# Layer-norm rows of the feed-forward norms spread by TensorE into PSUM, in a two-layer transformer trunk on one core

## The chip, the core and the metric

One core of a Trainium2 chip runs the whole program: TensorE (PE, with its weight loads as PEld), VectorE (DVE), ScalarE (ACT), GpSimd (POOL) and the DMA queue of SyncE (SP). The metric is the device time of one execution in microseconds (us), as the median of several runs.

## The reference

Input `x` has 512 tokens of 1024 features, in float32. There are two layers. Layer 0 mixes the tokens with a gated linear recurrence and a differential attention, layer 1 with a forgetting attention of 16 heads. What matters here is the frame around the mixers, the same in both layers:

```python
x = _layer_norm(ALPHA * x + mixer(x), ln1_g[l], ln1_b[l])
x = _layer_norm(ALPHA * x + _swiglu(x, ffn_w1[l], ffn_w2[l]), ln2_g[l], ln2_b[l])

def _layer_norm(x, g, b, eps=1e-5):
    mu = mean(x); var = mean((x - mu) ** 2)
    return (x - mu) * rsqrt(var + eps) * g + b
```

`ln1_g`, `ln1_b`, `ln2_g`, `ln2_b` are rows of 1024 numbers per layer. `_swiglu` has 2816 hidden features. So there are four layer norms, here called n1_0, n2_0 (layer 0, behind the mixer and behind the feed-forward part), n1_1 and n2_1. In the code, `norm` has them as n = 0, 1, 2, 3; the odd ones are the feed-forward norms.

## The kernel before

Tokens lie on the 128 partitions in four tiles (t = 0 to 3) of `x_res`, and features on the free axis. For every projection the activations are turned (feature on the partitions) by TensorE transposes into PSUM (`turn_tile`, L516), and each turned half tile is split into a rounded high part `xT_hi` by ScalarE (`split_hi`, L992) and a rest `xT_lo` by VectorE (`split_lo`, L1254). Weights come in chunks of up to 128x2048: SP loads a chunk into one of two raw buffers (`load`, L890), ScalarE rounds it into `w_hi` (L980), GpSimd makes the rest `w_lo` in pieces of 512 columns (L940), in a ring of three. Each product is three matmuls (`products`, L445 to L447). A chunk may be rounded when the chunk three before it has been used, and may be loaded when GpSimd is through with the chunk two before it.

The order of work on each engine is written out by hand; semaphores alone tie the engines together. PSUM banks 0 to 3 take the large products, in turn; banks 4 to 7 take transposes, attention and the products of gate and up (`h_buf`, banks 4 and 5). `open_bank` makes TensorE wait until the last reader of a bank has freed it.

Each layer ends its mixer with the projection `out{l}` and its feed-forward part with `down{l}`, both in two halves of 512 output columns. The first half is done chunk by chunk; VectorE adds it to `x_res` with `add_left` (L1434) and takes its statistics (L1435). The second half goes tile by tile in `tail_products`, and between tiles `norm_tail` places the transposes of the tiles already normed: in the n1 tails two tiles behind, in the n2_0 tail one behind. So that TensorE has work while the last tiles are normed, it also holds early pieces of the next stage: `early(0)` stands before the transposes of tile 3 and `early(1)` behind them. In the n1 tails these are the first halves of the first two gate/up products; in n2_0 they are two tiles of `foxq0` and the forget-gate product `fox_f`. `early(0)` needs tiles 0 and 1 turned and split.

VectorE does a norm tile in this order: `add_left` and statistics of the second half, aggregate (L1442), add epsilon (L1443), then `(x - mean) * gain` over 1024 columns (L1447), then it takes the root that ScalarE made meanwhile (Ln and Exp, L997 and L998), refines it with three operations on one column (L1450 to L1452), and does `x * r + bias` over 1024 columns (L1453). Behind tile t it splits tile t - 1.

The gain and bias rows lie in SBUF, broadcast to 128 partitions by DMA (512 KB each). For n1 they go to free parts of the arena, ahead of the `out{l}` chunks (L921). For n2 they go to `rows_ffn`, a part of the arena that holds hidden activations until chunk 8 of `down{l}` has been used. The SP queue waits for that use (`ffn_rows`, L905 and L907), ahead of the load of the chunk behind `down0`, and in layer 1 ahead of the output.

Of the kernel before, what the change touches and what calls it, by code (L numbers as in the profile page):

```python
# [123 lines left out]
def build(nc, w, out):  # L124
# [5 lines left out]
    with ExitStack() as ctx:  # L130
# [27 lines left out]
        level_mask = place("level_mask", [len(LEVELS), P], BF16, 2)  # L158
        small = place("small", [48], F32, 4)
# [38 lines left out]
        rows_ffn, _ = take("rows_ffn", [2, D], F32, 0)  # L198
        norm_rows = [rows_even, rows_ffn, rows_fox, rows_ffn]
# [35 lines left out]
        def named(*names):  # L235
            for n in names:
# [26 lines left out]

        n_masks = 2 + len(LEVELS)
# [10 lines left out]
                   for h in range(AH)]  # L275
        lam_loads = [(lam_rows[:, i * HD:(i + 1) * HD], w[n][0:1, :].to_broadcast([P, HD]))
# [133 lines left out]
        def _(pe):  # L410
# [121 lines left out]
            def norm_tail(tag, step, src_tiles, lag, early):  # L532

                def turn(t):

                    turn_tile(tag, t, x_res, lambda: pe.wait_ge(S["norm_done"], step * NT + t + 1),  # L540
                              4 + 2 * (t % 2))

                for t in range(NT):
                    src_tiles(t)
                    if early and t >= lag:
                        turn(t - lag)
                if early:
                    for t in range(NT - lag, NT - 1):
                        turn(t)
                    early(0)  # L550
                    turn(NT - 1)
                    early(1)
                    turned_tiles[0] += NT
# [70 lines left out]
            def swiglu(l):  # L624
# [18 lines left out]
                for i in range(6):  # L643
                    pe.wait_ge(S["h_lo"], l * NF + k0 + chunks[cs[i]][2] // 512)
                    drain(token_chunk(cs[i], "dve", hT_hi, hT_lo, k0, i == 0, (f"down{l}", 0) if i == 5 else False))
                    k0 += chunks[cs[i]][2] // 512
                k0 = 0
# [12 lines left out]
            def fox_start(i):  # L660
# [10 lines left out]
                acc = open_bank("fox_f", 4, "dve")  # L671
# [8 lines left out]
                used_with_bank(c, "fox_f")  # L680

# [202 lines left out]
        def _(sp):  # L884
# [18 lines left out]
            def ffn_rows(l):  # L903

                sp.wait_ge(*chunk_used[stage_chunks[f"down{l}"][8]])  # L905
                for i, name in enumerate(("ln2_g", "ln2_b")):
                    sp.dma_start(rows_ffn[:, i, :], w[name][l:l + 1, :].to_broadcast([P, D])).then_inc(rows_in[l], 16)  # L907

            for c in range(2, len(chunks)):
                if c == stage_chunks["down0"][-1] + 1:  # L910
                    ffn_rows(0)
                for l in range(DEPTH):
                    if c == chunk_at(f"out{l}"):
                        if l == 0:

                            sp.wait_ge(S["act_free"], 1)
                        else:

                            sp.wait_ge(S["fexp"], 3 * QUARTER)
                        for i, name in enumerate(("ln1_g", "ln1_b")):  # L920
                            sp.dma_start(norm_rows[2 * l][:, i, :], w[name][l:l + 1, :].to_broadcast([P, D])  # L921
                                         ).then_inc(rows_in[l], 16)
                load(c)
            ffn_rows(1)
# [307 lines left out]
        def _(dve):  # L1232
# [24 lines left out]

            def refine(r, var, tmp):
# [178 lines left out]
            def norm(tag, name, n):  # L1437

                for t in range(NT):
# [4 lines left out]
                    dve.wait_ge(rows_in[n // 2], 32 * (n % 2 + 1))  # L1444
                    gain, bias = (norm_rows[n][:, i, :] for i in range(2))
                    xs = x_res[:, t, :]
                    step(stt(xs, xs, st[:, 12:13], gain, ALU.subtract, ALU.mult))  # L1447
# [4 lines left out]
                    step(tt(r, r, tmp, ALU.mult))  # L1452
                    chain(stt(xs, xs, r, bias, ALU.mult, ALU.add), S["norm_done"])  # L1453
                    if t >= 1 and tag != "n2_1":
# [155 lines left out]
```

## Time and profile before

| | |
|---|---|
| median of 3 runs | 1483.52 us (1482.2 to 1485.66) |
| the profiled execution | 1485.66 us, of which 1483.9 us are its span |
| TensorE busy | 1398.3 us, 94% of the span |
| VectorE, ScalarE, GpSimd busy | 480.5, 499.9, 527.6 us |
| granted TensorE clock, mean | 0.968 of full speed |
| norms n1_0, n2_0, n1_1, n2_1 | end at about 345, 711, 1118 and 1481 us |

Times in rows are microseconds from the start of the span, unless marked ns. The ends of matmuls are modelled: the distance from start to start tells what one costs. A matmul of float32 operands stands in the trace as two instructions.

### The profile page before, as it was taken

What the parts mean: (1) busy time and instruction counts of PE and PEld (TensorE: products, weight loads), DVE (VectorE), ACT (ScalarE), POOL (GpSimd) and SP (SyncE); (2) the same over time, 40 slices, a digit from 0 to 9 for tenths busy, and PEclk for the clock granted to TensorE, in tenths of its full rate; (3) what the DMA queues carried; (4) which work ended last, traced back from release to release, by engine and by line L of the source; (5) the groups of instructions that cost most, each with busy time, mean ns of one, the idle gap of its engine ahead of it and who ended that gap; (6) DMA issues with size and microseconds to landing.
All of it is one profiled execution on the core that took longest, in us unless ns stands there. A gap on an engine that the chain in (4) does not pass through costs nothing.

```text
span 1483.9 us, 19200 instructions
## 1 busy us (share of the span) xinstructions
PE 1398.3 (94%) x7244; PEld 1174.8 (79%) x7244; DVE 480.5 (32%) x1120; ACT 499.9 (34%) x824; POOL 527.6 (36%) x421
## 2 busy tenths in 40 slices
PE   7999996799999999999899998889899999999997
PEld 6888874578888888887778887877679888888886
DVE  3366526553111111014536271533362111110005
ACT  4313236424223232112435554544323222323120
POOL 5421312044544445351342222202134454454450
PEclk9999998899999999999999999979799999999999
DMA  6311121022333233322232121012012323324231
GB/s 220 112 32 57 58 86 57 1 86 70 101 105 94 86 99 111 102 85 59 86 114 58 58 58 57 1 64 80 29 57 86 113 86 96 104 71 140 73 114 57
DMA packets 136891, 119.53 MB, mean 81 GB/s; under 512 B 5472, under 2 KB 112096, under 8 KB 136800
## 3 DMA queue, kind: packets, MB, share of 16 engines
q1 hardware_dynamic: 136800, 118.31, 25.6%
q8 instruction: 58, 0.95, 0.3%
q14 instruction: 33, 0.27, 0.1%
HBM read 116.20 MB, written 2.10 MB: 80 GB/s over the span
## 4 chain that ended last, share of the span: by engine, by line
PE 81%; DVE 8%; ACT 6%; issue 3%; POOL 1%; DMA 0%; ACTq 0%; DVEq 0%; POOLq 0%; SPq 0%
PE banks L445 24%; PE banks L447 24%; PE banks L446 24%; PE banks L856 2%; PE banks L874 2%; ACT w_hi L980 1%; PE banks L720 1%; PE banks L516 1%; PE banks L865 1%; ACT p_fox L1202 1%; POOL w_lo L940 1%; DVE small L1534 1%; DVE xT_lo L1254 1%; PE banks L820 1%; PE banks L787 1%
## 5 line engine op out<-in xcount | busy, mean ns | idle before, releaser
L940 POOL TENSOR_TENSOR w_lo<-w_raw,w_hi 128x512 fp32r<-128x512 f32 x417 | 527.3, 1297 | 920.2 <-ACT w_hi L980 920.2
L445 PE MATMUL banks<-xT_lo,w_hi 128*128 128x512 f32 (+2 forms) x928 | 344.9, 372 | 2.8 <-DVEq L1256 2.8
L447 PE MATMUL banks<-xT_hi,w_hi 128*128 128x512 f32 (+2 forms) x928 | 343.1, 370 | 0.0
L446 PE MATMUL banks<-xT_hi,w_lo 128*128 128x512 f32 (+2 forms) x928 | 342.9, 370 | 0.0
L980 ACT ACTIVATE w_hi<-w_raw 128x2048 fp32r<-128x2048 f32 (+1 forms) x107 | 200.0, 1869 | 201.3 <-PE banks L447 167.0
L445 PE MATMUL banks<-w_lo,xT_hi 128*128 128x512 f32 (+1 forms) x608 | 222.6, 366 | 11.4 <-ACT o_fox L1002 3.9
L447 PE MATMUL banks<-w_hi,xT_hi 128*128 128x512 f32 (+1 forms) x608 | 215.2, 354 | 0.0
L446 PE MATMUL banks<-w_hi,xT_lo 128*128 128x512 f32 (+1 forms) x608 | 214.7, 353 | 0.0
L445 PEld LDWEIGHTS banks<-xT_lo,w_hi 128*128 128x128 f32 (+1 forms) x928 | 173.9, 187 | 32.6 <-issue 3.5
L447 PEld LDWEIGHTS banks<-xT_hi,w_hi 128*128 128x128 f32 (+1 forms) x928 | 173.7, 187 | 29.7
L446 PEld LDWEIGHTS banks<-xT_hi,w_lo 128*128 128x128 f32 (+1 forms) x928 | 173.9, 187 | 29.5
L1472 DVE TENSOR_TENSOR banks<-silu_g,banks 128x512 f32<-128x512 f32 x44 | 30.6, 697 | 402.7 <-PE banks L447 402.7
L445 PE MATMUL banks<-w_lo,hT_hi 128*128 128x512 f32 x352 | 137.9, 392 | 3.6 <-POOL w_lo L940 3.6
L445 PEld LDWEIGHTS banks<-w_lo,xT_hi 128*128 128x128 f32 x608 | 119.8, 197 | 25.6 <-issue 12.7
L446 PE MATMUL banks<-w_hi,hT_lo 128*128 128x512 f32 x352 | 137.7, 391 | 0.0
L447 PE MATMUL banks<-w_hi,hT_hi 128*128 128x512 f32 x352 | 137.6, 391 | 0.0
L447 PEld LDWEIGHTS banks<-w_hi,xT_hi 128*128 128x128 f32 x608 | 119.2, 196 | 15.2
L446 PEld LDWEIGHTS banks<-w_hi,xT_lo 128*128 128x128 f32 x608 | 120.1, 198 | 13.1
L1144 ACT ACTIVATE silu_g<-banks 128x512 f32<-128x512 f32 x44 | 26.4, 599 | 306.7 <-PE banks L447 306.6
L1434 DVE SCALAR_TENSOR_TENSOR x_res<-x_res,banks 128x512 f32<-128x512 f32 x32 | 22.0, 688 | 236.0 <-PE banks L447 235.0
L445 PEld LDWEIGHTS banks<-w_lo,hT_hi 128*128 128x128 f32 x352 | 66.5, 189 | 18.2 <-issue 4.4
L447 PEld LDWEIGHTS banks<-w_hi,hT_hi 128*128 128x128 f32 x352 | 66.5, 189 | 13.9
(165 smaller groups left out, 1271.9 us busy)
## 6 DMA issues: line engine op xcount, KB each, us to landing
w_raw<-in_ffn_w_dram SPq DMA_DIRECT2D x92, 512.0 KB, 3.9
w_raw<-in_ffn_w_dram SPq DMA_DIRECT2D x20, 1024.0 KB, 5.0
w_raw<-in_fox_w_in_dram SPq DMA_DIRECT2D x16, 1024.0 KB, 5.8
w_raw<-in_even_w_in_dram SPq DMA_DIRECT2D x14, 1024.0 KB, 5.0
w_raw<-in_even_w_out_dram SPq DMA_DIRECT2D x4, 1024.0 KB, 5.1
w_raw<-in_fox_w_out_dram SPq DMA_DIRECT2D x4, 1024.0 KB, 6.4
x_res<-in_x_dram SPq DMA_DIRECT2D x4, 512.0 KB, 8.0
out_dram<-x_res SPq DMA_DIRECT2D x4, 512.0 KB, 2.6
```

Source lines behind the costliest of these rows:

```text
L445: mm(acc, l_hi, r_lo, start=first, stop=False)
L446: mm(acc, l_lo, r_hi, start=False, stop=False)
L447: return mm(acc, l_hi, r_hi, start=False, stop=final)
L516: ins = nc.tensor.transpose(acc[:, j * P:(j + 1) * P], src[:, t, f:f + P], ident[:, :])
L720: ins = mm(halves(acc[:, tok], z)[:, :, 1, :], k[:, tok], halves(q[:, tok], z)[:, :, 1, :], start=True, stop=True)
L856: mm(acc[:, 0:n], qA[0:HA, j % 2, h % 4, i * P:(i + 1) * P], kA[0:HA, j % 2, h % 4, 0:n], start=True, stop=False)
L874: ins = mm(acc[:, 0:HD], pT_fox[:, u % 2, j * P:(j + 1) * P], v_all[:, j, h * HD:(h + 1) * HD], start=j == 0, stop=j == i)
L940: ins = nc.gpsimd.tensor_tensor(w_lo[c % RING][:, a:a + n], w_raw[c % RAW][:, a:a + n], w_hi[c % RING][:, a:a + n].bitcast(F32), ALU.subtract)
L980: chain(fn(w_hi[c % RING][:, 0:size], w_raw[c % RAW][:, 0:size], ACT.Copy), hi_ready)
L1144: release(fn(silu_buf(j), acc[:, :], ACT.Silu), (f"up{l}", j, 0))
L1434: release(stt(xs, xs, ALPHA, full(key)[:, :], ALU.mult, ALU.add), key)
L1472: release(tt(h_buf(j), silu_buf(j), acc[:, :], ALU.mult), (f"up{l}", j, 1))
```

## The change

The gain and bias rows of the two feed-forward norms are no longer broadcast by DMA. Their four rows are loaded once, at the start of the program, into four partitions of a small tile `ln_rows`, behind the other constants and ahead of the four loads for lambda. In each layer TensorE then spreads the two rows over 128 partitions into PSUM banks 4 to 7 (`spread_rows`), between the two halves of `down{l}`: four float32 matmuls with a column of the identity, repeated 128 times, as the stationary operand. VectorE reads gain and bias from those banks and frees them behind the last tile. The transposes of the n2_0 tail go to banks 0 and 1, 0 and 1, 2 and 3, 4 and 5, and `fox_f` to bank 6. In `norm`, for all four norms, the operation with the gain now stands behind the root and its refinement.

```diff
+        ln_rows = place("ln_rows", [D], F32, 4)
...
+        rows = [w[n][l:l + 1, :] for l in range(DEPTH) for n in ("ln2_g", "ln2_b")]
...
+        consts += [(ln_rows[i:i + 1, :], row) for i, row in enumerate(rows)]
...
                     turn_tile(tag, t, x_res, lambda: pe.wait_ge(S["norm_done"], step * NT + t + 1),
-                              4 + 2 * (t % 2))
+                              (0, 0, 2, 4)[t] if step % 2 else 4 + 2 * (t % 2))
...
+                spread_rows(l)
                 k0 = 0
                 for i in range(6, 9):
...
-                acc = open_bank("fox_f", 4, "dve")
+                acc = open_bank("fox_f", 6, "dve")
...
+            def spread_rows(l):
+                for i in range(4):
+                    key = ("rows", l, i)
+                    acc = open_bank(key, 4 + i, "dve")
+                    row = 2 * l + i // 2
+                    sel = ident[0:2 * DEPTH, row:row + 1].to_broadcast([2 * DEPTH, P])
+                    close_bank(key, mm(acc[:, :], sel, ln_rows[0:2 * DEPTH, (i % 2) * 512:(i % 2) * 512 + 512],
+                                       start=True, stop=True))
...
-            def ffn_rows(l):
-
-                sp.wait_ge(*chunk_used[stage_chunks[f"down{l}"][8]])
-                for i, name in enumerate(("ln2_g", "ln2_b")):
-                    sp.dma_start(rows_ffn[:, i, :], w[name][l:l + 1, :].to_broadcast([P, D])).then_inc(rows_in[l], 16)
-
             for c in range(2, len(chunks)):
-                if c == stage_chunks["down0"][-1] + 1:
-                    ffn_rows(0)
...
-            ffn_rows(1)
...
+            def free_now(key):
+                s = freed["dve"][uses[key][0]]
+                counts[id(s)] = counts.get(id(s), 0) + 1
+                dve.sem_inc(s, 1)
...
                     chain(ts(st[:, 13:14], st[:, 13:14], 1e-5, None, ALU.add), S["ln_arg"])
-                    dve.wait_ge(rows_in[n // 2], 32 * (n % 2 + 1))
-                    gain, bias = (norm_rows[n][:, i, :] for i in range(2))
-                    xs = x_res[:, t, :]
-                    step(stt(xs, xs, st[:, 12:13], gain, ALU.subtract, ALU.mult))
                     dve.wait_ge(S["ln_done"], n * NT + t + 1)
                     r, tmp = st[:, 14:15], st[:, 15:16]
                     step(stt(tmp, r, r, st[:, 13:14], ALU.mult, ALU.mult))
                     step(ts(tmp, tmp, -0.5, 1.5, ALU.mult, ALU.add))
                     step(tt(r, r, tmp, ALU.mult))
+
+                    if n % 2:
+                        for i in range(4):
+                            full(("rows", n // 2, i))
+                        gain, bias = banks[:, 4:6, :], banks[:, 6:8, :]
+                    else:
+                        dve.wait_ge(rows_in[n // 2], 32)
+                        gain, bias = (mixer_rows[n // 2][:, i, :].rearrange("p (a b) -> p a b", a=2) for i in range(2))
+                    xs = x_res[:, t, :].rearrange("p (a b) -> p a b", a=2)
+                    step(stt(xs, xs, st[:, 12:13], gain, ALU.subtract, ALU.mult))
                     chain(stt(xs, xs, r, bias, ALU.mult, ALU.add), S["norm_done"])
+                    if t == NT - 1 and n % 2:
+                        for i in range(4):
+
+                            free_now(("rows", n // 2, i))
```

## Rows read from the trace of the kernel before

**Rows 1.** The page: the chain that ended last, by engine.
```profile
PE 81%; DVE 8%; ACT 6%; issue 3%; POOL 1%; DMA 0%; ACTq 0%; DVEq 0%; POOLq 0%; SPq 0%
```

**Rows 2.** Timeline of TensorE: start us, us, engine, line, operation. Float32 products, 512 columns.
```profile
229.90 1.13 PE L787 MATMUL banks<-bkT,bqT 64*128 64x512 f32 x4
230.96 0.29 PE L789 MATMUL banks<-diff_mask,ident_bf 128*128 128x128 bf16 x2
...
828.30 1.02 PE L856 MATMUL banks<-kA,qA 66*128 66x512 f32 x2
829.16 0.22 PE L858 MATMUL banks<-fox_mask,ident_bf 128*128 128x128 bf16 x1
```

**Rows 3.** Timeline of TensorE, between the halves of down0: matmuls of rounded operands.
```profile
620.18 0.39 PE L446 MATMUL banks<-w_hi,hT_lo 128*128 128x512 f32 x1
620.40 0.39 PE L447 MATMUL banks<-w_hi,hT_hi 128*128 128x512 f32 x1
```

**Rows 4.** Timeline of all engines, the last norm tile of n2_1.
```profile
1475.71 0.69 DVE L1434 SCALAR_TENSOR_TENSOR x_res<-x_res,banks 128x512 f32<-128x512 f32 x1 [3.03 <-PE banks L447]
...
1477.59 1.28 DVE L1447 SCALAR_TENSOR_TENSOR x_res<-x_res,stats,rows_ffn 128x1024 f32<-128x1024 f32 x1
...
1477.89 0.20 ACT L998 ACTIVATE stats<-stats 128x1 f32<-128x1 f32 x1
1478.91 0.22 DVE L1450 SCALAR_TENSOR_TENSOR stats<-stats 128x1 f32<-128x1 f32 x1
...
1479.55 1.28 DVE L1453 SCALAR_TENSOR_TENSOR x_res<-x_res,stats,rows_ffn 128x1024 f32<-128x1024 f32 x1
```

**Rows 5.** Groups by shape, VectorE: 1024 columns read from two banks; mean ns last.
```profile
L1409 DVE TENSOR_REDUCE small<-banks 128x2 f32<-128x1024 f32 x4 | 4.9, 1224 | 3.1 <-PE banks L789 3.1
```

**Rows 6.** Timelines of ScalarE and VectorE: the step from a root to its refinement.
```profile
729.09 0.20 ACT L998 ACTIVATE fox_ms<-fox_ms 128x4 f32<-128x4 f32 x1
...
729.39 0.16 DVE L1260 TENSOR_TENSOR fox_ms<-fox_ms 128x4 f32<-128x4 f32 x1 [0.64 <-ACT fox_ms L998]
```

**Rows 7.** Timeline of VectorE, tiles 2 and 3 of n1_1.
```profile
1106.63 1.28 DVE L1447 SCALAR_TENSOR_TENSOR x_res<-x_res,stats,rows_fox 128x1024 f32<-128x1024 f32 x1
1107.95 0.22 DVE L1450 SCALAR_TENSOR_TENSOR stats<-stats 128x1 f32<-128x1 f32 x1
...
1108.59 1.28 DVE L1453 SCALAR_TENSOR_TENSOR x_res<-x_res,stats,rows_fox 128x1024 f32<-128x1024 f32 x1
...
1113.54 2.29 DVE L1447 SCALAR_TENSOR_TENSOR x_res<-x_res,stats,rows_fox 128x1024 f32<-128x1024 f32 x1
```

**Rows 8.** Timelines of ScalarE and GpSimd beside them.
```profile
1106.93 0.20 ACT L998 ACTIVATE stats<-stats 128x1 f32<-128x1 f32 x1
...
1109.15 5.59 POOL L940 TENSOR_TENSOR w_lo<-w_raw,w_hi 128x512 fp32r<-128x512 f32 x4 [16.59 <-ACT w_hi L980]
```

**Rows 9.** Timeline of TensorE beside them: transposes of tile 2, early(0), transposes of tile 3.
```profile
1109.93 1.09 PE L516 MATMUL banks<-ident,x_res 128*128 128x128 f32 x8 [0.98 <-DVE x_res L1453]
1111.97 0.35 PE L445 MATMUL banks<-xT_lo,w_hi 128*128 128x256 f32 x1 [0.95 <-DVEq L1256]
1117.84 1.09 PE L516 MATMUL banks<-ident,x_res 128*128 128x128 f32 x8
```

**Rows 10.** Timelines of VectorE and TensorE in the n2_0 tail.
```profile
687.84 0.69 DVE L1434 SCALAR_TENSOR_TENSOR x_res<-x_res,banks 128x512 f32<-128x512 f32 x1 [3.07 <-PE banks L447]
...
687.57 1.03 PE L516 MATMUL banks<-ident,x_res 128*128 128x128 f32 x8
688.36 0.48 PE L445 MATMUL banks<-w_lo,hT_hi 128*128 128x512 f32 x1
...
707.80 0.36 PE L445 MATMUL banks<-w_lo,xT_hi 128*128 128x256 f32 x1 [1.06 <-POOL w_lo L940]
```

**Rows 11.** Timelines of SP and ScalarE: load and rounding of the chunk behind down0.
```profile
668.60 0.43 SPq L890 DMA_DIRECT2D w_raw<-in_fox_w_in_dram  x1
...
700.54 1.92 ACT L980 ACTIVATE w_hi<-w_raw 128x2048 fp32r<-128x2048 f32 x1
```

**Rows 12.** Timelines of SP, ScalarE and GpSimd at the start.
```profile
13.00 1.85 SPq L900 DMA_DIRECT2D gains<-in_hgrn_lb_logits_dram  x4
...
24.67 1.91 ACT L980 ACTIVATE w_hi<-w_raw 128x2048 fp32r<-128x2048 f32 x1 [7.19 <-DMA w_raw<-in_even_w_in_dram]
...
38.39 0.60 ACT L1002 ACTIVATE kT<-banks 128x512 f32<-128x512 f32 x1 [4.84 <-PE banks L447]
...
26.65 10.02 POOL L940 TENSOR_TENSOR w_lo<-w_raw,w_hi 128x512 fp32r<-128x512 f32 x8 [4.05 <-ACT w_hi L980]
```

**Rows 13.** Stretches: length, busy us (count) per engine, granted clock, DMA share, GB/s.
```profile
676.00:680.00 4.00, 4.00 (x12) 3.14 (x11) 0.35 (x1) 0.00 (x0) 0.00 (x0) 0.59 0.17 16
```

**Rows 14.** Timeline of TensorE: the wait in the down1 tail, and the same in down0.
```profile
1448.12 0.47 PE L445 MATMUL banks<-w_lo,hT_hi 128*128 128x512 f32 x1 [1.81 <-POOL w_lo L940]
...
674.96 0.47 PE L445 MATMUL banks<-w_lo,hT_hi 128*128 128x512 f32 x1 [1.81 <-POOL w_lo L940]
```

More of the change, by code:

```diff
@@ L197, in build @@
         assert 2 * D <= 4 * TS and e2 <= 3 * AH * TS + 2 * TS + 3 * P + 20 * P
-        rows_ffn, _ = take("rows_ffn", [2, D], F32, 0)
-        norm_rows = [rows_even, rows_ffn, rows_fox, rows_ffn]
+        mixer_rows = [rows_even, rows_fox]
         qA, e = take("qA", [2, 4, TS], F32, 0)
@@ L920, in _ @@
                         for i, name in enumerate(("ln1_g", "ln1_b")):
-                            sp.dma_start(norm_rows[2 * l][:, i, :], w[name][l:l + 1, :].to_broadcast([P, D])
+                            sp.dma_start(mixer_rows[l][:, i, :], w[name][l:l + 1, :].to_broadcast([P, D])
                                          ).then_inc(rows_in[l], 16)
                 load(c)
-            ffn_rows(1)
             o = out[0].rearrange("(t p) d -> p t d", p=P)
```

## The prediction, as put on record before the changed kernel ran

> **What bounds the kernel now.** I read the chain that ended last first: TensorE holds 81% of it [rows 1]. So time that is added to TensorE's own queue counts in full, unless TensorE would have waited at that point anyway. Time on another engine counts only where TensorE, or at the end the output, waits for it. Next I went through the timelines of the four norm tails, since the change touches nothing else in mid-program, and last through the start of the program, where constants are loaded. Between the halves of down0 TensorE goes from one matmul to the next in 0.22 us with no wait [rows 3]: nothing there hides added work. In the n1 tails VectorE is late: TensorE waits 0.98 us for the norm of tile 2 and 0.95 us for the splits behind it [rows 9]. In the n2 tails a tile of products is longer than a norm tile, and VectorE is idle 3.03 us before the last tile [rows 4]. The very end is VectorE's alone: the last norm tile, then the output.
>
> **The spread on TensorE (added).** There are four float32 matmuls per layer, eight in all, each with 512 moving columns and 4 rows. The trace has no such matmul with 4 rows. The nearest row is the fox score product, with 66 rows and 512 columns: its two instructions take from 828.30 to 829.16, 0.86 us [rows 2]. Float32 products with 64 rows ran in pairs: four instructions, two products, from 229.90 to 230.96, so 0.53 us each [rows 2]. I read this as two products on separate rows of the array, side by side; the four of the change all use the same four rows, so I take 0.86. Sum: 8 x 0.86 = 6.9 us, all on the path. The bounds are 8 x 0.53 = 4.2 us and, should rows not matter and each product cost only what a rounded matmul costs, 8 x 0.22 = 1.8 us [rows 3]. At half clock for the whole spread it would be 13.8 us. The waits on banks 4 to 7 are free: their last readers are the hidden activations, which TensorE has waited for before down starts. The weights stay ahead: the one wait in each down tail (1.81 us, for the last chunk [rows 14]) counts from the use of chunk 8, behind the spread, so the spread neither causes nor fills it.
>
> **The removed broadcasts.** SP no longer waits for chunk 8, and four transfers of 512 KB go. In layer 0 the load of the foxq0 chunk was issued at 668.60, but ScalarE rounds that chunk at 700.54, behind other work [rows 11]; a load some 5 us earlier meets a wait of 30 us. In layer 1 nothing but the output stands behind the rows. VectorE did not wait for the rows: the first operation with the gain follows at once. Gain: 0. It could reach 1.06 us at most, the wait for the weights of foxq0 [rows 10], if that hung on the load.
>
> **The four small loads at the start.** They stand ahead of the load of chunk 2. Four small loads took SP 1.85 us [rows 12]. ScalarE waits for that chunk until 24.67, so it and GpSimd go back 1.85 us: GpSimd, with chunks 2 and 3 together, from 36.7 to 38.5 [rows 12]. Its first half, chunk 2, is done at about 33.5. TensorE comes to chunk 2 when the last forget-gate group is through, at about 38.3, which the evacuation at 38.39 shows [rows 12]. So some 5 us cover it, and the cost is 0. Without that cover it would be 1.85 us.
>
> **The gain operation moved behind the root (all four norms).** Before, 1.28 us of VectorE ran beside ScalarE's root. Now VectorE idles until the root is there. In n1_1 the root is ready at 1106.93 + 0.20 = 1107.13; VectorE takes it 0.10 us later [rows 6]; the three small ones take 1108.59 - 1107.95 = 0.64 [rows 7]. The gain operation starts at 1107.87 instead of 1106.63, and the bias operation at 1107.87 + 1.32 = 1109.19 instead of 1108.59: 0.6 us per tile. The last tile of n2_1 gives the same: the root is ready at 1478.09, the bias operation starts at 1478.09 + 0.10 + 0.64 + 1.32 = 1480.15 instead of 1479.55 [rows 4]. That is 0.6 us straight on the end. In n2_0 VectorE has slack and it costs 0; without that slack, 0.6.
>
> **Gain and bias read from PSUM.** A sum with one input in PSUM takes 0.69 us for 512 columns [rows 4], and a reduce over 1024 columns in two banks 1.22 us [rows 5], against 1.28 for the operation with both in SBUF. I take 1.28 again. Bounds: twice 0.69 = 1.38, so 0.2 us more for two, and 1.22, so 0.1 less. The Trainium skill ("VectorE: DVE Perf Modes", section on the TRN2 errata) puts the fixed part of a VectorE operation at 120 cycles from PSUM against 58 from SBUF; by it the end would come 0.13 us later, and no row here separates the two. Three extra semaphore waits per tile I put at 0 to 0.2 us (successive operations that each wait follow within 0.04 us [rows 7]); the four releases stand behind the last norm, off the end.
>
> **Two more terms in n1: GpSimd.** In tile 3 of n1_1 the gain operation took 2.29 us instead of 1.28, while GpSimd worked [rows 7, 8]: both inputs in SBUF, GpSimd reading SBUF, a wait of 1.0 us until a piece was done. After the change that row is behind GpSimd's work and the wait goes, but it was not on the path, since early(0) lay over it. Now tile 2: GpSimd starts its pieces at 1109.15, which hangs on the root and not on the moved operation [rows 8]. The moved gain operation ends at 1107.87 + 1.28 = 1109.15, and the bias operation asks at 1109.19. So GpSimd, waiting already, gets in between, and the bias operation starts 1.0 us late. With the 0.6 the norm of tile 2 is 1.6 us late, and TensorE waits for it [rows 9]: early(0) and the transposes of tile 3 shift by 1.6. Behind them nothing gives it back. n1_0 has the same pattern: together 3.2 us. Without the collision it would be 1.2.
> The Trainium skill ("SBUF — State Buffer", "Who interferes with whom") says that a VectorE instruction with two SBUF inputs and a GpSimd instruction that reads SBUF exclude each other for the whole instruction, the later one blocking. By it up to a full piece, 5.59 / 4 = 1.4 us, could be lost, and in the n2 norms, with the rows in PSUM, none. The row of 2.29 us agrees.
>
> **Banks in the n2_0 tail.** The second half of the transposes of tile 0 goes to bank 1, which VectorE reads for tile 1 from 687.84 to 688.53. Before, that half would have started at about 687.97, halfway between 687.57 and 688.36 [rows 10]. It now starts at about 688.58: 0.6 us on TensorE. The transposes of tile 2 wait in the same way for bank 3, but a wait of 1.06 us for weights stands behind them and covers it [rows 10]. Tile 1's banks are split in time, and tile 3 needs the end of the norm anyway. What queues behind the new wait is tile 2's products, and through them everything later.
>
> **Sum.** 6.9 + 0.6 (end) + 3.2 (n1) + 0.6 (bank 1) = 11.3 us. On the profiled execution's span of 1483.9 this gives 1495.2, on its time of 1485.66, 1497.0; that execution is the slowest of the three shown, 2.1 above their median. On the median: 1483.5 + 11.3 = 1494.8 us, 0.8% more.
>
> **Rivals.**
> *GpSimd does not get in between in n1.* The two requests lie 0.04 us apart. Then n1 costs 1.2 instead of 3.2: 1492.8 us.
> *The 4-row matmuls are cheap.* For it speaks the pair at 0.53; against it that the single product with 66 rows is not. With 1.8 to 4.2 us instead of 6.9: 1489.7 to 1492.1 us.
> *The clock drops.* TensorE's idle before tile 2 of n1 grows from 1.0 to 2.6 us. A wait of 1.81 us in down0 was followed by 4 us at a granted clock of 0.59, between 1.2 and 2.4 GHz, a loss of 0.41 x 4 = 1.6 us [rows 13, 14]; the same wait in down1 was followed by no drop in that tail. One to two such drops give 1496.4 to 1498.0; if the spreads, with few rows at work, ran at half speed, 6.9 more, 1501.7.
> *Not slower: the removed traffic pays.* If foxq0's weights hung on their load, 1.06 us would come back, and the early load would have to pull the following chunks too. It decides only where it gives back more than 8.3 us, so that the rise falls under 0.2%. Or drops of the clock later in the program fall otherwise once everything is shifted: each was worth about 1.6 us, so seven would have to vanish. 1483.5 us as its time. The rows speak against both.
>
> **How the numbers follow.** Forecast 0.50; no collision 0.18; cheap matmuls 0.09; clock 0.17; not slower 0.06. The range leaves out the last and the far end of the clock case, and widens the cheap end by 1 us for the scatter of the runs: 1488.7 to 1500. What a measurement of this kernel can tell from no change is about 0.2%, 3 us. Slower 0.94, same 0.04, faster 0.02.
>
> **What would show it.** In the changed kernel's timeline: four float32 matmuls between the halves of each down, 0.86 us apart (if 0.5 or 0.2, the second rival); in n1, tile 2, a bias operation of about 2.3 us and TensorE's wait before its transposes at 2.6 us; the transposes of tile 0 in n2_0 in two groups, with a gap of 0.6; the last bias operation 0.6 us later against its `add_left`; no waits on the first chunks. I am wrong if TensorE's matmuls between the halves do not shift, or if a wait that I do not see here (a bank of the n2_0 tail, foxq0's weights) shrinks or grows by more than a microsecond.

## The result and the profile after

The changed kernel took 1503.12 us as the median of 4 runs (1502.59 to 1504.18), the one before, on the same chip, 1484.4 (4 runs, 1482.2 to 1485.66). The ratio is 1.0129, interval 1.0115 to 1.0141: 18.7 us slower by the medians. The forecast had been 1494.8, or 11.3 slower, with a range that ended at 1500. The direction was right; 7.4 us were not foreseen.

The chain that ended last still belongs to TensorE [rows 1]:
```profile
PE 82%; DVE 8%; ACT 6%; issue 3%; POOL 1%; DMA 0%; ACTq 0%; DVEq 0%; POOLq 0%; SPq 0%
```

**The spread.** Timeline of TensorE between the halves of down0, in the changed kernel, where [rows 3] had no foreign matmul:
```profile
646.00 0.39 PE L450 MATMUL banks<-w_hi,hT_hi 128*128 128x512 f32 x1
646.32 3.69 PE L693 MATMUL banks<-ln_rows,ident 4*128 4x512 f32 x8
649.94 0.50 PE L448 MATMUL banks<-w_lo,hT_hi 128*128 128x512 f32 x1
650.28 0.39 PE L449 MATMUL banks<-w_hi,hT_lo 128*128 128x512 f32 x1
```
Eight instructions (four products) lie in the group of 3.69. From the rounded matmul at 646.00 to the second one behind the group (650.28) it is 4.28 us; two rounded matmuls would have taken 0.45. The spread adds 3.83 us, not 4 x 0.86 = 3.44. The 0.4 us between the two lie at the edges of the group: its first instruction starts 0.32 us behind its predecessor instead of 0.22, the group takes 3.62 us from its first start to the next rounded matmul instead of 8 x 0.43 = 3.44, and that matmul holds the next back to 0.34.

**The clock behind it.** Stretches of the changed kernel (length, busy time and count of PE, PEld, DVE, ACT, POOL, then granted clock, DMA share, GB/s): behind the spread of layer 0, behind that of layer 1, and behind the wait in the down1 tail:
```profile
650.00:652.00 2.00, 2.00 (x8) 1.63 (x8) 0.00 (x0) 0.00 (x0) 2.00 (x2) 0.75 0.00 0
652.00:654.00 2.00, 2.00 (x6) 1.51 (x6) 0.00 (x0) 0.00 (x0) 1.47 (x2) 0.50 0.00 0
654.00:656.00 2.00, 2.00 (x10) 1.61 (x9) 0.00 (x0) 0.00 (x0) 0.00 (x0) 0.90 0.67 146
...
1430.00:1432.00 2.00, 2.00 (x6) 1.58 (x5) 0.00 (x0) 0.00 (x0) 2.00 (x3) 0.50 0.00 0
...
1466.00:1468.00 2.00, 2.00 (x8) 1.58 (x7) 0.00 (x0) 0.00 (x0) 0.00 (x0) 0.70 0.00 0
1468.00:1470.00 2.00, 2.00 (x7) 1.54 (x6) 0.18 (x1) 0.00 (x0) 0.00 (x0) 0.50 0.00 0
1470.00:1472.00 2.00, 2.00 (x10) 1.66 (x9) 1.56 (x4) 0.27 (x2) 0.00 (x0) 0.95 0.00 0
```
Each of these stretches is called a drop below. TensorE is busy throughout, yet runs at 1.2 instead of 2.4 GHz for a while. The first stretch loses 2 x (0.25 + 0.50 + 0.10) = 1.7 us of work at full clock, and so do the two others (the second has 0.81, 0.50 and 0.84 from 1428 to 1434). The first two have no match in the kernel before; the third stands in place of the one in [rows 13], which has gone.

**The n1 norms.** Timelines of VectorE, GpSimd and TensorE around tile 2 of n1_1 [rows 7 to 9]:
```profile
1116.44 0.22 DVE L1456 SCALAR_TENSOR_TENSOR stats<-stats 128x1 f32<-128x1 f32 x1 [0.63 <-ACT stats L1003]
1117.08 1.28 DVE L1468 SCALAR_TENSOR_TENSOR x_res<-x_res,stats,rows_fox 128x1024 f32<-128x1024 f32 x1
1118.39 2.30 DVE L1469 SCALAR_TENSOR_TENSOR x_res<-x_res,stats,rows_fox 128x1024 f32<-128x1024 f32 x1
...
1118.36 5.95 POOL L945 TENSOR_TENSOR w_lo<-w_raw,w_hi 128x512 fp32r<-128x512 f32 x4 [16.59 <-ACT w_hi L985]
...
1120.75 1.09 PE L519 MATMUL banks<-ident,x_res 128*128 128x128 f32 x8 [2.61 <-DVE x_res L1469]
```
All of it is as predicted: 0.63 us of idle for the root, GpSimd's pieces 0.03 us ahead of the bias operation, that operation at 2.30 us, TensorE's wait at 2.61 (0.98 before). What the forecast did not carry is the next view, the stretch behind that wait, and the one behind the wait of 2.96 us at the same place in n1_0:
```profile
1122.00:1124.00 2.00, 1.35 (x6) 1.39 (x7) 1.78 (x4) 0.00 (x0) 2.00 (x2) 0.51 0.00 0
...
344.00:346.00 2.00, 2.00 (x11) 2.00 (x10) 1.21 (x6) 1.40 (x4) 0.39 (x1) 0.50 0.12 32
```
What these two cost can be read from TensorE's timeline, from the start of tile 2's transposes to that of tile 3's, with the same matmuls between them in both kernels. Before, it is 1117.84 - 1109.93 = 7.91 us [rows 9], and the same in n1_0. In the changed kernel it is 9.78 in n1_0 and 8.96 in n1_1:
```profile
340.84 1.97 PE L519 MATMUL banks<-ident,x_res 128*128 128x128 f32 x8 [2.96 <-DVE x_res L1469]
350.62 1.03 PE L519 MATMUL banks<-ident,x_res 128*128 128x128 f32 x8
...
1129.71 1.03 PE L519 MATMUL banks<-ident,x_res 128*128 128x128 f32 x8
```
So the two drops cost 1.87 + 1.05 = 2.9 us, on top of the longer waits.

**Bank 1 and the end.** TensorE in the n2_0 tail [rows 10], then VectorE at the end [rows 4]:
```profile
697.30 0.60 PE L519 MATMUL banks<-ident,x_res 128*128 128x128 f32 x4
698.32 0.66 PE L519 MATMUL banks<-ident,x_res 128*128 128x128 f32 x4 [0.42 <-DVE x_res L1444]
...
1494.63 0.69 DVE L1444 SCALAR_TENSOR_TENSOR x_res<-x_res,banks 128x512 f32<-128x512 f32 x1 [2.43 <-PE banks L450]
...
1499.07 1.28 DVE L1469 SCALAR_TENSOR_TENSOR x_res<-x_res,stats,banks 128x1024 f32<-128x1024 f32 x1
```
The transposes of tile 0 stand in two groups, 1.02 us apart from start to start where the groups of [rows 10] had about 0.4: 0.6 us. The last bias operation starts 4.44 us behind its `add_left`, before 3.84: 0.6 us.

### The profile page after: what moved, and what is told of

It reads as the page before. It is cut to its first block, busy times and chain, and to the rows that moved or that the text cites. A ratio compares the mean times of both kernels' runs of the same rounds, so it can differ in the third digit from the quotient of the medians.

```text
span 1503.4 us, 19247 instructions
## 1 busy us (share of the span) xinstructions
PE 1413.9 (94%) x7260; PEld 1184.6 (79%) x7260; DVE 480.4 (32%) x1120; ACT 499.9 (33%) x824; POOL 528.4 (35%) x421
## 4 chain that ended last, share of the span: by engine, by line
PE 82%; DVE 8%; ACT 6%; issue 3%; POOL 1%; DMA 0%; ACTq 0%; DVEq 0%; POOLq 0%; SPq 0%
PE banks L448 24%; PE banks L450 24%; PE banks L449 24%; PE banks L870 2%; PE banks L888 2%; PE banks L734 1%; ACT w_hi L985 1%; PE banks L879 1%; POOL w_lo L945 1%; ACT p_fox L1207 1%; PE banks L519 1%; DVE xT_lo L1259 1%; PE banks L834 1%; DVE small L1554 1%; PE banks L801 1%
## 5 line engine op out<-in xcount | busy, mean ns | idle before, releaser
L448 PEld LDWEIGHTS banks<-w_lo,xT_hi 128*128 128x128 f32 x608 | 120.1, 197 | 24.8 <-issue 11.9
```

The lines of the kernel that those rows point to most:

```text
L448: mm(acc, l_hi, r_lo, start=first, stop=False)
```

## The experiments

Each kernel was timed against the kernel before on the same chip; "+" is the difference of medians to it; the ends of a ratio's interval, turned into microseconds, lie 1.3 to 3.3 us to either side. Theory: the change's own work costs what was predicted, and the rest is the clock, which drops behind matmuls with few rows at work and behind the longer waits in n1.

**1. The gain operation first again, all else as changed.**
```diff
                     chain(ts(st[:, 13:14], st[:, 13:14], 1e-5, None, ALU.add), S["ln_arg"])
+                    if n % 2:
...
+                    xs = x_res[:, t, :].rearrange("p (a b) -> p a b", a=2)
+                    step(stt(xs, xs, st[:, 12:13], gain, ALU.subtract, ALU.mult))
                     dve.wait_ge(S["ln_done"], n * NT + t + 1)
...
                     step(tt(r, r, tmp, ALU.mult))
-                    if n % 2:
...
-                    step(stt(xs, xs, st[:, 12:13], gain, ALU.subtract, ALU.mult))
                     chain(stt(xs, xs, r, bias, ALU.mult, ALU.add), S["norm_done"])
```


> The changed kernel, with the gain operation of all four norms back ahead of the root. Theory A (the miss is the clock: each long wait or sparse stretch of TensorE is followed by 3 to 6 us at half clock): the waits before the transposes of tile 2 in n1 fall from 2.96 and 2.61 us to about 1, the half-clock stretches behind them go, the bias operation of tile 2 takes 1.28 us again; 3.4 + 2.6 us in n1 and 0.6 us at the end come back, 6.6 us in all: 12.1 us above the kernel before. Theory B (the late root costs only its own time, and the extra comes from elsewhere): only 1.6 + 1.6 + 0.6 = 3.8 us come back, 14.9 us above the kernel before.


Measured: 1494.83 us, ratio 1.0074 (1.0054 to 1.0095), +11.8. The order costs 18.7 - 11.8 = 6.9 us, give or take some 3, of which 3.3 are the two longer waits in n1 and 0.6 the end. The 3.0 that are left agree with the 2.9 read from the trace for the two drops. Theory B's 14.9 lies outside the interval of 8.0 to 14.1. Its trace has TensorE's wait in n1_0 back at its old length, and no drop behind it:
```profile
335.98 1.09 PE L519 MATMUL banks<-ident,x_res 128*128 128x128 f32 x8 [1.31 <-DVE x_res L1469]
```
```profile
336.00:340.00 4.00, 3.21 (x26) 3.00 (x27) 3.49 (x7) 0.70 (x3) 4.00 (x4) 1.00 0.00 0
...
644.00:648.00 4.00, 4.00 (x12) 3.08 (x12) 0.00 (x0) 0.00 (x0) 2.79 (x3) 0.57 0.11 7
```
The drop behind the spread (644 to 648) stays. The one behind the wait for chunk 8, which both kernels have once, is missing in this trace, and the drop behind the second spread is twice as long (3.4 us of work), so these two cancel.

**2. The spreading matmuls one at a time**, behind chunks 5, 6, 7 and 8 of the down.
```diff
-                spread_rows(l)
                 k0 = 0
+                spread_rows(l, 0)
                 for i in range(6, 9):
                     drain(token_chunk(cs[i], "dve", hT_hi, hT_lo, k0, i == 6, False))
+                    spread_rows(l, i - 5)
```


> The changed kernel, with the four spreading matmuls of a layer one at a time, behind chunks 5, 6, 7 and 8 of down, instead of all four behind chunk 5. Theory A (3.6 us in a row with four rows at work drop the clock): each takes 0.9 us as before, but no stretch at half clock follows; about 1.6 us per layer come back, 3.3 in all, 15.4 us above the kernel before. Theory B (the half-clock stretches behind the spreads are chance or hang on the sum of the work): nothing comes back, 18.7 us above.


Measured: 1497.75 us, ratio 1.0102 (1.008 to 1.0124), +14.7. No drop is left in either down. The interval of 11.9 to 18.4 us only just leaves out theory B's 18.7; the missing drops are what decides. The total hit theory A's 15.4, but partly by luck, as TensorE's timeline shows:
```profile
1421.19 0.39 PE L450 MATMUL banks<-w_hi,hT_hi 128*128 128x512 f32 x1
1421.51 1.12 PE L694 MATMUL banks<-ln_rows,ident 4*128 4x512 f32 x2
...
1422.90 0.40 PE L449 MATMUL banks<-w_hi,hT_lo 128*128 128x512 f32 x1
```
From 1421.19 to 1422.90 it is 1.71 us, so one product alone adds 1.71 - 0.45 = 1.26, four of them 5.0 instead of 3.83 in a group. In return the last one lies over most of the wait of 1.81 us for chunk 8 (longest wait on GpSimd now 0.6), and the drop that before had behind it is missing too.

**3. All 128 rows at work.** Each gain or bias row is loaded into 32 partitions.
```diff
-        consts += [(ln_rows[i:i + 1, :], row) for i, row in enumerate(rows)]
+        consts += [(ln_rows[32 * i:32 * i + 32, :], row.to_broadcast([32, D])) for i, row in enumerate(rows)]
...
-                    sel = ident[0:2 * DEPTH, row:row + 1].to_broadcast([2 * DEPTH, P])
+                    sel = ident[:, 32 * row:32 * row + 1].to_broadcast([P, P])
-                    close_bank(key, mm(acc[:, :], sel, ln_rows[0:2 * DEPTH, (i % 2) * 512:(i % 2) * 512 + 512],
+                    close_bank(key, mm(acc[:, :], sel, ln_rows[:, (i % 2) * 512:(i % 2) * 512 + 512],
```


> The changed kernel, with each of the four rows loaded into 32 partitions and all 128 rows at work in the spreading matmuls (the column of the identity picks one). Same four matmuls in the same place. If few rows at work are what drops the clock: the 3.6 us stay, the half-clock stretches behind them go, 15.4 us above the kernel before. If it is the float32 operands, or the one non-zero row: no change, 18.7 us above.


Measured: 1498.13 us, ratio 1.0101 (1.0083 to 1.012), +15.1. Same place, same columns, same number of instructions, other rows; TensorE's timeline, and the stretch behind it:
```profile
643.61 0.39 PE L450 MATMUL banks<-w_hi,hT_hi 128*128 128x512 f32 x1
643.83 3.59 PE L693 MATMUL banks<-ln_rows,ident 128*128 128x512 f32 x8
...
647.50 0.39 PE L449 MATMUL banks<-w_hi,hT_lo 128*128 128x512 f32 x1
```
```profile
648.00:652.00 4.00, 4.00 (x19) 3.32 (x18) 0.00 (x0) 0.00 (x0) 3.11 (x3) 1.00 0.00 0
```
No drop, in either layer. The group adds 3.89 - 0.45 = 3.44 us, which is 4 x 0.86: the 0.4 us at the edges is gone too, though the operands are float32 as before. So it goes with the few rows and not with the type of the operands.

**4. GpSimd later in n1.** ScalarE rounds the second gate/up chunk only behind the split of tile 1, so that GpSimd starts behind tile 2's bias operation.
```diff
-                    if t == NT - 2 and lag == 2:
-                        hi_upto(after + 2)
                     if t >= 1 and tag != "n2_1":
                         split_hi(tag, t - 1)
-                    if t == NT - 2 and lag == 1:
+                    if t == NT - 2:
                         hi_upto(after + 2)
```


> The changed kernel, with ScalarE rounding the second gate/up chunk behind the split of tile 1 instead of ahead of it in the n1 tails, so that GpSimd starts some 3 us later. If the bias operation of tile 2 is held up by GpSimd's piece: it takes 1.28 instead of 2.3 us, TensorE's waits before the transposes of tile 2 fall by 1.0 us, to about 1.9 and 1.6, which may or may not be short enough to keep the clock up: 2 us come back without the clock, 4 to 5 with it; 14 to 17 us above the kernel before. If the long bias operation has another cause it stays at 2.3 us, and the time at 18.7 above.


Measured: 1501.18 us, ratio 1.0121 (1.0101 to 1.014), +18.1, so the median moved by only 0.6 us. Its interval of 15.0 to 20.8 holds most of the 14 to 17 that was expected, so the time alone does not tell whether anything came back. Tile 2's bias operation is at 1.28 us again, so the collision is what made it 2.3. But a drop still follows TensorE's wait in both n1 norms, as VectorE's and TensorE's timelines and two stretches show:
```profile
336.04 1.28 DVE L1467 SCALAR_TENSOR_TENSOR x_res<-x_res,stats,rows_even 128x1024 f32<-128x1024 f32 x1
337.38 1.45 PE L519 MATMUL banks<-ident,x_res 128*128 128x128 f32 x8 [1.93 <-DVE x_res L1467]
346.07 1.10 PE L519 MATMUL banks<-ident,x_res 128*128 128x128 f32 x8
...
1117.38 1.09 PE L519 MATMUL banks<-ident,x_res 128*128 128x128 f32 x8 [1.56 <-DVE x_res L1467]
1126.59 1.03 PE L519 MATMUL banks<-ident,x_res 128*128 128x128 f32 x8
```
```profile
338.00:340.00 2.00, 1.55 (x8) 1.18 (x7) 1.60 (x4) 0.28 (x1) 1.65 (x2) 0.50 0.00 0
1120.00:1122.00 2.00, 2.00 (x11) 2.00 (x11) 1.30 (x4) 0.88 (x3) 2.00 (x3) 0.50 0.00 0
```
By these rows the waits are 1.03 and 1.05 us shorter than in the changed kernel, and the two drops cost 0.78 + 1.30 = 2.1 us instead of 2.9. The n1 norms gave back 2.9 us in this trace; that the median shows only 0.6 is not explained. The collision moved to tile 3's small operations, which took 0.54 to 1.02 us instead of about 0.2.

**5. The kernel before, with the spread alone**: four float32 matmuls of 4 rows and 512 columns of the identity into banks 4 to 7, with no reader.
```diff
+                spread_dummy()
                 k0 = 0
                 for i in range(6, 9):
```


> The kernel before, with four float32 matmuls of 4 rows and 512 columns between the halves of each down, into banks 4 to 7; nobody reads them, all else is as before. Theory A (few rows at work, then half clock): the own time 2 x 3.6 = 7.2 us, and behind each spread a stretch at half clock that costs 1.6 us: +10.4 us. Rival B (the clock falls only by the change's other waits, or by chance): +7.2 us, no stretch at half clock at 650 or 1430 us. Since the drop that before has behind the wait of 1.81 us can go or come, each has +-1.6.


Measured: 1496.4 us, ratio 1.0091 (1.0074 to 1.0108), +13.4. More than either expected, though 11.0 us, the interval's lower end, is near 2 x 3.83 + 2 x 1.7 = 11.1. Both drops are there with nothing else of the change; in layer 0:
```profile
642.00:644.00 2.00, 2.00 (x6) 1.08 (x5) 0.00 (x0) 0.00 (x0) 2.00 (x3) 0.71 0.00 0
644.00:646.00 2.00, 2.00 (x6) 1.58 (x5) 0.00 (x0) 0.00 (x0) 2.00 (x2) 0.50 0.00 0
646.00:648.00 2.00, 2.00 (x10) 1.60 (x9) 0.00 (x0) 0.00 (x0) 0.14 (x1) 0.94 0.26 17
```
Rival B, the clock by other waits or by chance, falls. Some 2 us of the median I can't place: matmul by matmul against the kernel before, the two spreads with their drops cost 5.45 and 5.50 us in the trace.

**6. The kernel before, with the gain operation behind the root.**
```diff
-                    dve.wait_ge(rows_in[n // 2], 32 * (n % 2 + 1))
-                    gain, bias = (norm_rows[n][:, i, :] for i in range(2))
-                    xs = x_res[:, t, :]
-                    step(stt(xs, xs, st[:, 12:13], gain, ALU.subtract, ALU.mult))
                     dve.wait_ge(S["ln_done"], n * NT + t + 1)
...
                     step(tt(r, r, tmp, ALU.mult))
+                    dve.wait_ge(rows_in[n // 2], 32 * (n % 2 + 1))
+                    gain, bias = (norm_rows[n][:, i, :] for i in range(2))
+                    xs = x_res[:, t, :]
+                    step(stt(xs, xs, st[:, 12:13], gain, ALU.subtract, ALU.mult))
```


> The kernel before, with the gain operation behind the root in all four norms, rows in SBUF by DMA as before. Theory A (the order alone makes the waits of 2.6 to 3.0 us in n1, and these make the clock fall): own time 2 x 1.6 + 0.6 = 3.8 us, and two stretches at half clock of 1.5 us: +6.8 us. Rival B (the drops in n1 need the rest of the change): +3.8 us. Rival C (with the rows in SBUF the n2 norms collide with GpSimd too): more than 8 us, and a gain or bias operation above 2 us in n2.


Measured: 1491.33 us, ratio 1.0056 (1.0041 to 1.0071), +8.3: theory A, on its high side. In both n1 norms tile 2's bias operation took 2.31 us and a drop follows; n1_1's lasts longer than in the changed kernel:
```profile
1112.00:1116.00 4.00, 3.20 (x17) 3.00 (x15) 2.92 (x8) 1.00 (x3) 2.78 (x3) 0.56 0.01 3
1116.00:1120.00 4.00, 4.00 (x24) 4.00 (x23) 3.68 (x5) 0.60 (x1) 0.00 (x0) 0.59 0.88 259
```
The operations of the n2 norms stayed at 1.285 us, so rival C falls; GpSimd did not work while they ran. In this trace the waits and the end cost 3.9 us and the two drops, read as above between the transposes, 0.35 + 2.51 = 2.9. The drop of 1.6 in down0 is missing, which leaves 5.2, below the interval of 6.1 to 10.5.

**7. Both cures in the changed kernel** (the edits of 1 and 2).

> The changed kernel with both cures: the gain operation ahead of the root again, and the spreading matmuls one by one behind chunks 5 to 8. If the two parts are independent, 18.7 - 6.9 - 4.0 = +7.8 us against before, which is the spread's own 8 x 0.86 and the 0.6 of the bank, and no stretch at half clock is left that before does not have. If the drops only move to another wait: +10 us or more.


Measured: 1493.46 us, ratio 1.0066 (1.0048 to 1.0084), +10.4. No drop in the down tails, none behind n1's tile 2. The expectation took the spread at 0.86 a product; at 1.26 it is 10.1, with 0.6 for the bank and 2.7 less of waiting for GpSimd (4.7 before, 2.0 here) 8.0 us, inside the interval of 7.1 to 12.5, below the median. Against the trace of before, the drop of 1.6 us in down0 has gone too, which leaves 6.4, just outside it.

**8. The kernel before, with the down tails woven**: `tail_products` goes by pieces (tile, chunk), and the first chunk of tile 1 stands ahead of the last of tile 0 (0 to 2 are chunks 6 to 8).
```diff
-                    for n, (c, k0) in enumerate(parts):
+                    if acc_open and t == 0:
+                        order = [(0, 0), (0, 1), (1, 0), (0, 2)]
+                    elif acc_open and t == 1:
+                        order = [(1, 1), (1, 2)]
+                    else:
+                        order = [(t, n) for n in range(len(parts))]
+                    for u, n in order:
+                        piece(u, n)
```


> The kernel before, without the change: in the second half of each down the first two chunks of tile 1 stand between the second and the third chunk of tile 0, so that TensorE has work while GpSimd makes the rest of the last chunk. If the two waits of 1.81 us and the drop of the clock behind one of them (1.6 us) are what they cost: 1.81 x 2 + 1.6 = 5.2 us less, 0.9965 of before. If the clock falls elsewhere instead: 3.6 less. If the chunk behind waits in the same way (the next rounding hangs on a use that is now later): no change.


(The expectation speaks of two chunks of tile 1; the edit puts only the first one ahead.) Measured: 1478.26 us, ratio 0.9964 (0.9951 to 0.9977), 4.8 us less than before: the first of the three cases. The two waits of 1.81 us [rows 14] are gone, and the drop [rows 13] with them. By the view of TensorE's waits (total, times, longest), GpSimd is now waited for this long, against 4.7 us in three times before:
```profile
PE banks L445 <- POOL w_lo L948: 1.5, 2, 1.1
```

**9. The kernel before, with the four small loads at the start.**
```diff
+        consts += [(ln_rows[i:i + 1, :], row) for i, row in enumerate(rows)]
```


> The kernel before, with the four small loads of the rows at the start and nothing else; nobody reads them. Theory A (as predicted, the start has some 5 us of cover): within 0.5 us of before. Rival B (the step of 2.1 us that the changed kernel shows at 141 us comes from the later loads at the start): +2 us. Rival C (later loads set the mixer's pace in another way): more than 2 us.


Measured: 1485.13 us against 1485.28, ratio 1.0005 (0.9989 to 1.0021). The start is free, as predicted. The interval is -1.6 to 3.1 us, so rival B's 2 us is not shut out by the time alone. The trace settles it: the step of about 2 us at 141 us is a longer stretch at half clock in the mixer, from 134 to 142 us where the kernel before had 129 to 134, and run 8, which has no such loads, shows the same stretch. It does not come from the loads.

**10. The kernel before, with a spread of rounded matmuls**: eight per layer, 4 rows, 512 columns of `hT_hi`, no reader.
```diff
+                for i in range(8):
+                    mm(psum[4 + i // 2][:, :], hT_hi[0:4, i, 0:P], hT_hi[0:4, i, :], start=i % 2 == 0, stop=i % 2 == 1)
```


> The kernel before, with eight matmuls of rounded operands, 4 rows and 512 columns, between the halves of each down, into banks 4 to 7, without a reader: what TensorE would issue if the rows were spread as a rounded high part and a rest. Own time 16 x 0.22 = 3.5 us. Theory A (a stretch of 1.8 us with 4 rows at work is too short to bring the clock down, as the single float32 matmuls of 0.86 us were): +3.5 us, no half clock behind them. Rival B (it falls as behind the 3.6 us): +3.5 and two drops of 1.6: +6.7 us.


Measured: 1489.47 us, ratio 1.0033 (1.0018 to 1.0048), +4.2. TensorE's timeline and a stretch in layer 0:
```profile
637.93 0.39 PE L447 MATMUL banks<-w_hi,hT_hi 128*128 128x512 f32 x1
638.25 2.11 PE L686 MATMUL banks<-hT_hi 4*128 4x512 f32 x8
...
640.63 0.40 PE L446 MATMUL banks<-w_hi,hT_lo 128*128 128x512 f32 x1
```
```profile
642.00:644.00 2.00, 2.00 (x6) 1.56 (x5) 0.00 (x0) 0.00 (x0) 2.00 (x2) 0.50 0.00 0
```
Theory A of this run was wrong: two microseconds with 4 rows at work were enough for the drop, and float32 is not needed for it. Each group adds 640.63 - 637.93 - 0.45 = 2.25 us where eight rounded matmuls in the stream take 8 x 0.226 = 1.81, so the 0.4 us at the edges is here as well, without any float32. With two drops of 1.7 and without the one of 1.6 that before has behind the wait for chunk 8, the ledger gives 4.5 + 3.4 - 1.6 = 6.3 us, inside the interval of 2.7 to 7.1 but above the median.

**11. The changed kernel with both cures and the weave** (edits of 1, 2 and 8).

> The changed kernel with both cures and with tile 1's first chunk ahead of tile 0's last one in the down tails. The wait for the last chunk is already down to 0.6 us there, since a spreading matmul lies over it, so at most 1.2 us less than with the cures alone: +7 us if the cures' sum of 7.8 is right, +9 us if their measured 10.4 is. The kernel before with the same weave had -4.8; so the spread would stay 12 us behind.


Measured: 1490.64 us, ratio 1.0042 (1.0028 to 1.0055), +5.4 by the medians, 6.2 by the ratio: as expected or a little better.

**12. The changed kernel with the gain first, full rows in one group, and the weave** (edits of 1, 3 and 8).

> The changed kernel with the gain operation first, the spreading matmuls on 128 rows and in one group again, and the down tails woven. By the ledger so far: 2 x 3.44 us of TensorE for the spreads (measured start to start in the run with full rows), 0.6 for the bank, and the weave's 4.8 back: 6.9 + 0.6 - 4.8 = +2.7 us against before, and no stretch at half clock in the four norm tails. Rival (the clock needs the spacing, not the rows, or falls elsewhere when the waits move): +2.7 and two drops of 1.7: +6.1 us, no better than the 6.2 of the version with the spreads apart.


Measured: 1486.85 us against 1485.06, ratio 1.0011 (1.0002 to 1.002), +1.8: the ledger's 2.7 lies in the interval of 0.3 to 3.0 us, the rival's 6.1 far outside. It is the best form of the change, some 17 us ahead of the change as made, and the clock stays at 1.00 behind the spread and through the down tail:
```profile
650.00:654.00 4.00, 4.00 (x19) 3.31 (x18) 0.00 (x0) 1.92 (x1) 1.01 (x1) 1.00 0.69 262
676.00:684.00 8.00, 8.00 (x37) 6.63 (x36) 0.38 (x1) 0.00 (x0) 3.78 (x4) 1.00 0.09 8
```
The fastest kernel of all is run 8, without the change.

## Why the prediction was wrong

The step that failed is the rival "The clock drops". It allowed one or two drops of 1.6 us, only behind n1's longer wait, and gave them 0.17; for the spread it asked only whether the clock would fall during it. What happened is one drop behind each of four places, two n1 waits and two spreads, 6.3 us in all. The forecast's sum put the clock at nothing, and the range stopped short of it. Beside it, one term was mis-sized: the spreads took 7.7 us of TensorE's own time instead of 6.9.

The ledger of the 18.7 us, from the trace of the changed kernel; that the drops belong to the change is shown by runs 1, 3, 5 and 6:

| | predicted | measured |
|---|---|---|
| spreads, TensorE's own time | 6.9 | 2 x 3.83 = 7.7 |
| n1: late root and collision | 3.2 | 1.63 + 1.65 = 3.3 |
| bank 1 in n2_0 | 0.6 | 0.6 |
| end | 0.6 | 0.6 |
| drops behind the spreads | 0 | 2 x 1.7 = 3.4 |
| drops behind the n1 waits | 0 | 1.87 + 1.05 = 2.9 |
| start, removed broadcasts | 0 | 0 |
| sum | 11.3 | 18.5 |

That the sum meets the median this closely is partly luck: the four executions of the kernel before lie 3.5 us apart (28 others of it, in run 9, up to 9.8), and in the mixers, which the change does not touch, this trace differs from that of before by 1.2 us in total.

- **Price of the spread.** Right to choose the row of 0.86 and not the pair at 0.53; the "cheap matmuls" rival is dead. The product in the group costs that, 0.43 us from instruction to instruction. What was missed is 0.4 us at the edges of each group, which no row had been read for. It is not the passage between operand types: the group of float32 products with 128 rows does not have it (run 3, 3.44 us), the group of rounded ones with 4 rows does (run 10, 2.25 instead of 1.81). It comes with the passage from 128 rows to 4 and back. Run 2, with four such passages a layer, paid it four times.
- **GpSimd in n1.** Right, by 0.03 us (1118.36 against 1118.39), in both n1 norms, and proved by run 4, where GpSimd came later and the operation fell back to 1.28. The Trainium skill ("SBUF — State Buffer", "Who interferes with whom") has a VectorE instruction with two SBUF inputs contend with a GpSimd instruction that reads SBUF, and one with at most one such input not; the trace agrees: 2.30 us in n1 with both inputs in SBUF, while an `add_left` with one input in PSUM took its usual 0.69 at 1122.48, with GpSimd at work until 1124.3. The n2 norms are no test of it. GpSimd did not work while they ran, and in run 6, with all rows in SBUF, they stayed at 1.285.
- **Gain and bias from PSUM.** The choice of 1.28 was right: the eight gain and eight bias operations from PSUM have a mean of 1280 and 1281 ns, the gain operations of n1_0 from SBUF, which met no GpSimd, 1284 (groups by shape):
```profile
L1469 DVE SCALAR_TENSOR_TENSOR x_res<-x_res,stats,banks 128x1024 f32<-128x1024 f32 x8 | 10.2, 1281 | 0.3
L1468 DVE SCALAR_TENSOR_TENSOR x_res<-x_res,stats,banks 128x1024 f32<-128x1024 f32 x8 | 10.2, 1280 | 0.4
L1468 DVE SCALAR_TENSOR_TENSOR x_res<-x_res,stats,rows_even 128x1024 f32<-128x1024 f32 x4 | 5.1, 1284 | 0.1
```
An estimate from the cycle table of the Trainium skill ("VectorE: DVE Perf Modes", the section on the TRN2 errata) has the PSUM form 0.06 us slower; the measurement decides, there is no such difference here.
- **Bank 1, the end, the start, the removed broadcasts.** As predicted. The start has its own run (9). That the removed broadcasts are worth nothing was not tried by itself: it is argued from the ledger, which closes without them to within the scatter.
- **The clock.** Behind the spreads it is shown: the drop comes with the dummy spread alone (run 5) and goes with the rows filled (run 3), with nothing moved, and with the products spaced (runs 2 and 7). Behind n1 it is shown that the order of operations brings it (runs 1 and 6). That it is the length of TensorE's wait rests on a comparison and is not shown by an edit of its own: over the fourteen kernels, waits of 0.97 to 1.33 us at this place (18 of them) were followed by no drop, waits of 1.56 to 2.96 us (10, in the changed kernel and runs 2, 3, 4 and 6) by one each time.
- **What stays open.** Run 5 is some 2 us above its ledger, run 7 2 to 4 above its own, run 6 some 3, and run 4's median did not give back what its trace did. Why matmuls with few rows, or a longer wait, bring the clock down is not shown either, only that they do. Whether the wait of 1.81 us for chunk 8 brings a drop changes from kernel to kernel: it did in layer 0 before and in runs 4, 5 and 9, in layer 1 after, and in neither in runs 1, 3, 6 and 10. The even mixer's low stretches vary too. Where the clock falls in code that the change doesn't touch was not predictable from one profile, and a single profile is not good to better than 2 to 3 us for that reason.

## What to carry to other kernels

Price a matmul that is squeezed into a dense stream by two things: its pitch from start to start, and how many rows of the array it uses. Few rows cost twice here, 0.4 us at the edges of a group and a drop behind it; a one-row broadcast on TensorE was cheaper with the row loaded into all partitions. When a change lengthens a wait of TensorE from about 1 us to 1.6 or more, as it did here, allow for a stretch at half clock behind each such wait, besides the wait itself: in n1 it cost 0.4 to 2.5 us of time (changed kernel, runs 2, 3, 4 and 6). Look for what ends the wait rather than only for whose time grows: run 4 removed the delay of the bias operation, and the drops stayed, while a reordering of four pieces of work (run 8) took 4.8 us off the kernel before.

## What the hardware showed unexpectedly

- TensorE that is busy without a gap can still lose its clock: behind 3.6 us of float32 products with 4 rows (changed kernel, runs 1, 4 and 5) and behind 2.0 us of rounded ones (run 10). In the changed kernel it fell about 1 us after the group in layer 0, and with the first matmul behind it in layer 1 (1429.05, the next at 1429.49). With 128 rows, or with one product of 1.1 us at a time, it did not fall.
- A group of four float32 products of 512 columns adds 3.83 us with 4 rows and 3.44 with 128; a single one with 4 rows adds 1.26. Eight rounded ones with 4 rows add 2.25 us instead of 1.81. In each case with 4 rows it is 0.4 us more than the pitch inside the group gives.
- Each of these drops was worth 1.7 us of full-clock work, or twice that (3.4 behind n1_0's wait in the changed kernel, behind n1_1's in run 6 and behind the second spread in run 1). Behind a spread TensorE has work without a gap and the time grows by all of it. In n1 it partly waits anyway, and the time grew by less, 1.87 and 1.05 us in the changed kernel.
